# One-hot rows as bf16 pairs with the gates in three parts, and eight staging places for the streamed expert tiles

## What is computed

```python
q = (xf @ wq).reshape(n, PEER_HEADS, 2, PEER_HALF)
s = jnp.einsum('nhpd,hpkd->nhpk', q, subkeys)
s_top, i_top = lax.top_k(s, PEER_TOPK)
...
gate = jax.nn.softmax(best_s, axis=-1)
h = jnp.einsum('nd,nhkd->nhk', xb, u[eb])
coef = gb * jax.nn.gelu(h, approximate=False)
out = jnp.einsum('nhk,nhkd->nd', coef, v[eb])
```

## Time and profile before

| | |
|---|---|
| three timed runs | 2138.67 to 2146.58 us, median 2142.24 |
| profiled execution, its own time | 2145.48 us |
| its span in the trace | 2143.8 us |
| TensorE busy with matmuls | 1939.0 us, 90% |
| TensorE weight loads (beside the matmuls) | 1649.7 us, 77% |
| VectorE busy | 1605.5 us, 75% |
| ScalarE busy | 762.3 us, 36% |
| GpSimd busy | 582.9 us, 27% |
| moved by DMA | 416.49 MB, mean 194 GB/s |

### The profile page before, as it was taken

How to read it: one execution, slowest core, us unless ns; L and a number is a source line. 1 busy time by engine, 2 the same in 40 slices (tenths; PEclk the granted TensorE clock), 3 DMA queues, 4 the chain that set the end, 5 groups by cost and what they waited for, 6 DMA issues and landing times.

```text
span 2143.8 us, 33321 instructions
## 1 busy us (share of the span) xinstructions
PE 1939.0 (90%) x12866; PEld 1649.7 (77%) x12866; DVE 1605.5 (75%) x2822; ACT 762.3 (36%) x1114; POOL 582.9 (27%) x403
## 2 busy tenths in 40 slices
PE   5889998889998989999999999799999999997793
PEld 4879875359953479999999999778787778887682
DVE  6288993324553379999899999777787778797898
ACT  3222554422210044443455555333333333332231
POOL 2312342000000055545501000232222222265561
PEclk9989998878998989999999999999999999998997
DMA  3211231010050054444676767799999999899994
GB/s 121 79 50 60 95 111 39 1 41 3 4 197 0 0 192 137 127 135 149 211 253 236 246 240 244 275 336 323 344 334 325 313 343 339 293 370 333 369 347 154
DMA packets 173716, 416.49 MB, mean 194 GB/s; under 512 B 13952, under 2 KB 89216, under 8 KB 170384
## 3 DMA queue, kind: packets, MB, share of 16 engines
q1 hardware_dynamic: 119728, 256.16, 35.6%
q0 software_dynamic: 36864, 134.23, 17.3%
q10 hardware_dynamic: 16992, 24.26, 3.1%
HBM read 363.08 MB, written 51.51 MB: 193 GB/s over the span
## 4 chain that ended last, share of the span: by engine, by line
DVE 36%; PE 19%; DMA 6%; issue 2%; ACT 1%; SPq 0%; DVEq 0%; ACTq 0%
PE ps L1978 16%; DVE h_tok L1561 6%; DVE hot_hl L2104 5%; DVE w_hl L2111 4%; DMA w_staged<-in_stream 3%; DMA w_staged<-in_v 3%; DVE h1T L2100 3%; DVE hot L2102 3%; PE ps L1894 3%; DVE is_place L2060 1%; DVE gathered_rows L1552 1%; DVE is_place L2055 1%; PE ps L1898 1%; DVE coef_hl L2141 1%; DVE picks L2063 1%
## 5 line engine op out<-in xcount | busy, mean ns | idle before, releaser
L1978 PE MATMUL ps<-w_hl,coef_hl 128*128 128x512 f32 x2304 | 543.4, 396 | 30.4 <-DVE coef_hl L2141 30.3
L1978 PEld LDWEIGHTS ps<-w_hl,coef_hl 128*128 128x128 f32 x2304 | 434.7, 190 | 134.0 <-DVE coef_hl L2141 40.5
L1894 PE MATMUL ps<-h_hl,w_hl 128*128 128x384 f32 (+1 forms) x2304 | 451.6, 348 | 41.5 <-ACT h1T L1870 18.7
L1894 PEld LDWEIGHTS ps<-h_hl,w_hl 128*128 128x128 f32 x2304 | 412.0, 191 | 56.0 <-ACT w_hl L1825 33.8
L1825 ACT ACTIVATE w_hl<-w_staged 128x1024 fp32r<-128x1024 f32 x221 | 234.7, 1062 | 411.6 <-PE ps L1978 205.9
L1542 POOL DMA_INDIRECT gathered_rows<-in_u_rows,pick_index x128 | 141.5, 1106 | 575.0 <-DVE pick_hidden L1552 565.1
L2111 DVE TENSOR_TENSOR w_hl<-w_staged,w_hl 128x1024 fp32r<-128x1024 f32 x208 | 251.7, 1220 | 19.4 <-ACT w_hl L1825 19.4
L1898 PE MATMUL ps<-h_hl,w_hl 128*128 128x384 f32 (+1 forms) x1152 | 230.4, 341 | 0.0
L1542 POOL DMA_INDIRECT gathered_rows<-in_v,pick_index x128 | 164.1, 1282 | 168.1 <-DVE h_tok L1561 116.8
L1898 PEld LDWEIGHTS ps<-h_hl,w_hl 128*128 128x128 f32 x1152 | 204.2, 188 | 5.0
L1765 POOL TENSOR_TENSOR w_hl<-w_staged,w_hl 128x1024 fp32r<-128x1024 f32 x64 | 163.5, 2557 | 138.4 <-ACT w_hl L1790 113.9
(11 more groups left out here) (312 smaller groups left out, 2451.5 us busy)
## 6 DMA issues: line engine op xcount, KB each, us to landing
w_staged<-in_stream SPq DMA_DIRECT2D x144, 512.0 KB
w_staged<-in_v SPq DMA_DIRECT2D x128, 512.0 KB
dense_gates<-lot SPq DMA_DIRECT2D x24, 1024.0 KB, 4.8
gates<-dense_gates SPq DMA_DIRECT2D x16, 1536.0 KB
w_staged<-in_w_in_t SPq DMA_DIRECT2D x40, 512.0 KB, 3.5
parked_gelu<-h1T ACTq DMA_DIRECT2D x102, 192.0 KB
h1T<-parked_gelu SPq DMA_DIRECT2D x102, 192.0 KB
branch_gates<-h1T ACTq DMA_DIRECT2D x16, 256.0 KB, 2.0
```

Of the source, the lines that this page charges most:

```text
L1894: nc.tensor.matmul(ps[:, bank, 0:width], w_hl[:, j % RING, 0, P * k:P * (k + 1)], h_hl[:, part, k, lo:SEQ], start=(k == 0 and part == 0), ...
L1978: last = nc.tensor.matmul(ps[:, 2 + 2 * t + half, :], coef_hl[:, k % HLS, c, P * t:P * (t + 1)], w_hl[:, s % RING, v, 512 * half:512 * (ha ...
```

## The change

Two things are changed, both in `peer`.

The one-hot rows become bf16. `picks_b` holds the keys in bf16, `count128` holds each number from 0 to 127 twice, and the rows of two tokens are interleaved: in `[key, 2]` the innermost pair is two tokens. The gate is split by VectorE into three bf16 parts instead of two float32r parts, so that a four has 12 matmuls instead of 8 and the product with the gate writes 1536 elements for each partition instead of 1024. TensorE reads one token's row with a step of two elements.

```diff
-                    for part in range(2):
-                        last = nc.tensor.matmul(ps[:, 4 + q, P * n:P * (n + 1)], hot2[:, q, n, :],
-                                                hot1_hl[:, q, part, n, :], start=(part == 0), stop=(part == 1))
+                    for part in range(PARTS3):
+                        last = nc.tensor.matmul(ps[:, 4 + q, P * n:P * (n + 1)], hot2[:, q, n // 2, :, n % 2],
+                                                hot1[:, q, part, n // 2, :, n % 2],
+                                                start=(part == 0), stop=(part == PARTS3 - 1))
...
-            dve.wait_ge(gate_high, 1)
-            v_.tensor_tensor(gate_hl[:, 1, :], picksT[:, 2, :], gate_hl[:, 0, :].bitcast(F32), ALU.subtract
-                             ).then_inc(gate_low, 1)
-            dve.wait_ge(gate_low, 1)
+            by_four = gateT[:, :].rearrange("p (u n) -> p u n", n=FOUR)
+            for part in range(PARTS3):
+                v_.tensor_copy(gate_parts[:, :, part, :], by_four).then_inc(gate_split, 1)
+                dve.wait_ge(gate_split, 2 * part + 1)
+                if part < PARTS3 - 1:
+                    v_.tensor_tensor(by_four, by_four, gate_parts[:, :, part, :], ALU.subtract).then_inc(gate_split, 1)
+                    dve.wait_ge(gate_split, 2 * part + 2)
...
-                count = count128[:, :].unsqueeze(1).broadcast_to([P, FOUR, P])
+                count = count128[:, :, :].unsqueeze(1).broadcast_to([P, 2, P, 2])
+                pairs = lambda x: picks_b[:, x, now].rearrange("p (m n) -> p m n", n=2).unsqueeze(2).broadcast_to([P, 2, P, 2])
...
+                v_.tensor_tensor(is_key[:, u % 2], count, pairs(0), ALU.is_equal).then_inc(compared, 1)
+                v_.tensor_tensor(hot2[:, r], count, pairs(1), ALU.is_equal)
                 dve.wait_ge(compared, u + 1)
...
+                part_pairs = gate_parts[:, u, :, :].rearrange("p c (m n) -> p (c m) n", n=2)
+                v_.tensor_tensor(hot1[:, r].rearrange("p c m k n -> p (c m) k n"),
+                                 is_key[:, u % 2].unsqueeze(1).broadcast_to([P, PARTS3, 2, P, 2]),
+                                 part_pairs.unsqueeze(2).broadcast_to([P, 2 * PARTS3, P, 2]), ALU.mult
                                  ).then_inc(hot_ready, 1)
```

```diff
+    DEEP = 2 * RING
...
+    def place_of(s):
+
+        return s % RING if s < QUERIES + PARKED else (s - QUERIES - PARKED + RING) % DEEP
...
+        stage = [staged[:, j, :] for j in range(RING)] + [free[:, 1024 * j:1024 * (j + 1)] for j in (1, 3, 0, 2)]
...
-                if s < STREAMED:
-                    sp.wait_ge(late_low, s - RING - BY_POOL + 1)
...
+                j = place_of(s)
+                if j < RING:
+                    sp.wait_ge(late_low, before_in_place(s) - BY_POOL + 1)
+                elif s >= QUERIES + PARKED + DEEP:
+                    sp.wait_ge(late_low, s - DEEP - BY_POOL + 1)
+                sp.dma_start(stage[j], source(s) if s >= QUERIES + PARKED else a["stream"][s]).then_inc(landed[j], 16)
...
-            for k in range(COEFS):
-                load_parked(k)
+            load_from(FIRST_BEHIND + RING, QUERIES + PARKED)
             for j in range(2):
                 sp.wait_ge(lot_stored[j], 16 * (LOTS // 2))
             load_gates(0)
-            for s in range(FIRST_BEHIND, QUERIES + PARKED):
-                load_late(s + RING)
+            for k in range(COEFS):
+                load_parked(k)
+
+            load_from(QUERIES + PARKED, QUERIES + PARKED + 3)
+            for j in range(2):
+                sp.wait_ge(act_parked[j], 16 * (PARKED // 2 + 1))
+            load_from(QUERIES + PARKED + 3, QUERIES + PARKED + DEEP)
             for k in range(EXPERT_KEYS):
                 if k + LEAD in U_AT:
-                    load_late(U_AT[k + LEAD] + RING)
-                load_late(V_AT[k] + RING)
+                    load_from(U_AT[k + LEAD] + DEEP, U_AT[k + LEAD] + DEEP + 1)
+                load_from(V_AT[k] + DEEP, V_AT[k] + DEEP + 1)
```

More of the change, by code:

```diff
@@ L1607, in expert_of, with before_in_place @@
         return s // PER_HEAD * (PER_HEAD - 2) + (s % PER_HEAD - 2) if s < TOPK_TILES else s - QUERIES
+    def place_of(s):
+        return s % RING if s < QUERIES + PARKED else (s - QUERIES - PARKED + RING) % DEEP
+    def before_in_place(s):
+        return s - DEEP if s >= QUERIES + PARKED + DEEP else max(
+            n for n in range(QUERIES + PARKED) if n < s and n % RING == place_of(s))
+    landings = {}
+    for s in range(STREAMED):
+        landings[s] = 1 + sum(place_of(n) == place_of(s) for n in range(s))
     def freed_by(s):
@@ L1660, in peer @@
             lot = sb("lot", [P, 2, P, LOT], at=second)
-            hot1_hl = sb("hot1_hl", [P, RING, 2, FOUR, P], F32R, at=second)
-            hot2 = sb("hot2", [P, RING, FOUR, P], F32R, at=second)
+            hot1 = sb("hot1", [P, RING, PARTS3, 2, P, 2], BF16, at=second)
+            hot2 = sb("hot2", [P, RING, 2, P, 2], BF16, at=second)
+            is_key = sb("is_key", [P, 2, 2, P, 2], BF16, at=second)
         with ExitStack() as third:
@@ L1665, in peer @@
             coef_hl = sb("coef_hl", [P, HLS, 2, DENSE], F32R, at=third)
+            coefs = sb("coef", [P, COEFS, DENSE], at=third)
+            coef = [coefs[:, j, :] for j in range(COEFS)]
             stats, mv, std, rstd = (sb("stats2", [P, NT, 2, 6], at=third), sb("mv2", [P, NT, 2], at=third),
@@ L1671, in peer @@
         rows_landed, rows_order = sem("rows_landed"), sem("rows_order")
-        landed = [sem(f"w_landed{j}") for j in range(RING)]
+        landed = [sem(f"w_landed{j}") for j in range(DEEP)]
         h_high, h_low = sem("h_high"), sem("h_low")
@@ L1700, in load_late, with load_from @@
             def load_late(s):
-                if s < STREAMED:
-                    sp.wait_ge(late_low, s - RING - BY_POOL + 1)
-                    sp.dma_start(staged[:, s % RING, :], source(s) if s >= QUERIES + PARKED else a["stream"][s]
-                                 ).then_inc(landed[s % RING], 16)
+                j = place_of(s)
[4 more added lines that the diff above has]
+                sp.dma_start(stage[j], source(s) if s >= QUERIES + PARKED else a["stream"][s]).then_inc(landed[j], 16)
+            def load_from(first, end):
+                for s in range(first, min(end, STREAMED)):
+                    load_late(s)
             def load_gates(i):
@@ L1728, in _ @@
             for n in range(LOTS):
-                for s in range(FIRST_LOT + TILES_A_LOT * n, FIRST_LOT + TILES_A_LOT * (n + 1)):
-                    load_late(s + RING)
+                first = FIRST_LOT + TILES_A_LOT * n + RING
+                load_from(first, min(first + TILES_A_LOT, QUERIES + PARKED))
                 sp.wait_ge(four_copied, 4 * (n + 1))
                 sp.dma_start(dense[n], lot[:, n % 2, :, :].rearrange("p k n -> p (k n)")).then_inc(lot_stored[n % 2], 16)
-            for k in range(COEFS):
-                load_parked(k)
+            load_from(FIRST_BEHIND + RING, QUERIES + PARKED)
             for j in range(2):
@@ L1760, in _ @@
             nc.gpsimd.iota(count16[:, :], [[1, K]], 0, 0, allow_small_or_imprecise_dtypes=True).then_inc(counted, 1)
-            nc.gpsimd.iota(count128[:, :], [[1, P]], 0, 0, allow_small_or_imprecise_dtypes=True).then_inc(counted, 1)
+            nc.gpsimd.iota(count128[:, :, :], [[1, P], [0, 2]], 0, 0, allow_small_or_imprecise_dtypes=True).then_inc(counted, 1)
             def low(s, j):
@@ L1822, in high_of @@
                     what, n = freed_by(s)
[L1823 removed]
+                    act.wait_ge(landed[place_of(s)], 16 * landings[s])
                     act.wait_ge(tile_done if what == "tile" else sum_done, n)
[L1825 removed]
+                    nc.scalar.activation(w_hl[:, s % RING, 0, :], stage[place_of(s)], ACT.Copy).then_inc(w_high, 1)
             def expert(s, behind=False):
@@ L2110, in low @@
                     dve.wait_ge(w_high, s + 1)
-                    v_.tensor_tensor(w_hl[:, s % RING, 1, :], staged[:, s % RING, :],
+                    v_.tensor_tensor(w_hl[:, s % RING, 1, :], stage[place_of(s)],
                                      w_hl[:, s % RING, 0, :].bitcast(F32), ALU.subtract).then_inc(late_low, 1)
```

23 lines of the change are left out of this document (7 added, 16 removed).

## The result

The changed kernel takes 2083.85 us (median of 4 runs, 2077.34 to 2091.07) against 2144.41 us before in the same comparison; the ratio is 0.9718, 95% interval 0.9675 to 0.9762. Medians here are of fast runs alone, which leaves out one run of `two_parts`, at 2099.90 us.

The account below looks back on a forecast made before the run. Lots bound by VectorE with TensorE close, sums nearly filled by DMA; 2145.5 - 19 (lots) - 15 (order and places) = 2111.5, less 3.2 for the profiled execution's excess over the median: 2108 us, range 2084 to 2161.

Parts of the forecast that it names:

- VectorE's four: VectorE's three instructions a four in the lots: 1.53 us instead of 2.34 if 16-bit pairs pass in one tick, else 2.87.
- TensorE's price p: Time of one bf16 one-hot matmul in the lots: 65 ns, between 53 and 108; lots 278.9 us against 298.25, -19 us.
- Rival B: In the lots, bf16 weights load no faster than float32r, 108 ns a matmul: lots +30 us, total 2157; chance 0.25.
- The order behind the lots: Behind the lots, tiles 116 and 117 load first; first v tile late next, about 1395; sums start some 7 us earlier.
- The eight places: Four more staging places cover late tiles in the sums; with the earlier start, -15 us, range -28 to +3.
- The ceiling of 14.8 + 19 us: The most the sums could gain: 14.8 us in the parked keys and some 19 in the fresh keys.
- the 2 MB that fill the places: Loads that fill the added places in the sums, taken as 6 us off the possible gain.
- The mechanism of the places: In the sums, a gate block ahead in the queue makes a tile late; four more places give 17 us of cover.
- Rival D: In the sums, waiting moves from tiles to gates, so the places bring nothing: 2123 us, +-4; chance 0.15.
- VectorE's busy share in the lots: Sign in the lots: VectorE busy under 80%, against 297.1 of 298 us before.
- the DMA share of the fresh keys: Sign in the sums of the fresh keys: the DMA share rises to 0.97, from 0.93.

Follow-up runs that it names:

- two_parts: The changed kernel with the gate in two bf16 parts, the third part left out: 2065.28 us, ratio 0.963.
- token_major: The changed kernel with the bf16 rows of a token side by side instead of two tokens interleaved: 2163.4 us, ratio 1.0081.
- bf16_only: The kernel before with only the bf16 rows added, keeping four staging places and the old order of loads: 2115.15 us, ratio 0.9846.
- more_dots: The changed kernel with two dot products of gathered rows in each lot instead of one: 2061.53 us, ratio 0.9633.
- gates_together: bf16_only with each block of gates in four pieces, all issued together at the place of the old load: 2110.41 us, ratio 0.9828.

## Why the prediction was wrong in size

- **VectorE's four** (1.53 us) was right: 1.55, with pairs; and 2.87 without them, seen in token_major. The lots were then TensorE's, as the step said.
- **TensorE's price p** was mis-sized. I took 65 ns, half of the 108 before and some 10 for the step of two, for which I had no row. The half came true (loads 97 ns instead of 192, pace 57 instead of 108); the step costs under 2 ns. Whether the load is what set the 108 and sets the 57 is not shown: both operands changed their type at once, and 57 is also what 128 columns cost at the tile's 0.46 ns a column (59). 1152 x 8 ns = 9 us, the difference between -19 and -29 in the lots. Rival B (108 ns) is refuted. The Trainium skill's page "TensorE: Matmul & The Clock Gate", section "Back-to-back issue gap", was weighed with its 81 ns for a stream of loads and matmuls; the runs show 57, and the measurement decides. Its section "Weight-path perf modes", by which weights that are not FP32 load about twice as fast, agrees with 192 to 97 ns.
- **The order behind the lots** failed. That the first tile of v would be late next was right, and more tiles are done before the stall. But it was to be there some 27 us behind the end of the lots (1395), and ScalarE had it after 30.6; the sums started 3 us earlier instead of 7, and bf16_only has 2 of these 3 with the old order. With float32r rows the new order made the stage 2 us longer.
- **The eight places** were mis-sized most: -15 of a range ending at -28, measured -32 in the three stages together, and -31 in the sums when they came alone. The ceiling of 14.8 + 19 us was right. What failed was to take 6 us off it for the 2 MB that fill the places, and then to choose -15 out of the range with no term that gives it. The bytes cost no such time, since 346 GB/s, read in the 39 us of the behind stage, is not what DMA gives in the sums: over the whole of the parked keys it gives 349 to 351. Even at 346 the prediction's own 417 us for these bytes lay under TensorE's 419. Here the range failed too: its lower end of 2084 counts the places at -25, though their own range went to -28. That the time missed it by only 0.15 us is luck. Had I taken the ceilings alone, the sum would have been 2142 - 19 - 34 = 2089, and with the measured p 2079.
- **The mechanism of the places** was right, and the experiments sharpen it: what was to be covered is the block of gates ahead of the tiles, and four places with spread gates do as well (2082.74 us).
- **Rival D** had the mechanism of the queue right and its effect wrong: gates do stand in order with the tiles, but VectorE's wait for them went only from 12.1 to 13.5 us.
- Of what the profile was to show, VectorE's busy share in the lots (86%, under 80 foreseen) and the DMA share of the fresh keys (0.95, not 0.97) came out otherwise; the fresh keys stood at VectorE's work, as more_dots shows.

## What to carry to other kernels

When a tile of a deep, regular stream is late at regular distances, look at what else is issued on its queue just before: a large load in spread pieces did for nothing what four more buffers did. When two engines are within a few per cent of each other, price the work of both before and after, and afterwards ask what the one set free can take over. In the two-input instructions of this kernel bf16 paid on VectorE only where the innermost dimension of every operand really steps; a pair of tokens side by side was enough.

## What the runs showed of the hardware

- A two-input VectorE instruction with all operands bf16 takes, from start to start, 0.33 us for 512 and 0.87 us for 1536 elements with innermost rows of two, and 0.60 and 1.67 us if the innermost element of one input is repeated.
- 128 columns of weights load in 97 ns as bf16 and in 192 as float32r; short matmuls of 128 columns, with both operands of that type, follow at 57 and 108 ns. A step of two bf16 elements on both operands costs less than 2 ns (55 ns without it).
- A tile of v issued behind 1.5 MB of gates on the same queue is late whether the gates are one load or four: ScalarE waits 23 times, 87.4 us, in bf16_only and 24 times, 89.8 us, in gates_together, and 2 times, 7.2 us, when the same four loads are spread over four steps.
- TensorE passed the float32r matmuls of the sums at two paces with no wait between them, 133 or 130 in 30 us, both at a granted clock of 1.00; what decides is not known.
